# A hybrid two-block network on one core: the second block's projections written between the levels of its gated recurrence

## The reference

```
h = concatenate([meta, x])                       # 16 + 256 rows
q_pre, f_pre, i_pre, og_pre, lx, ly, ga, gb = split(rmsnorm(h) @ w_in)
# branch a: gated recurrence, 4 heads of 128
f = lb + (1 - lb) * sigmoid(f_pre);  k = (1 - lb) * sigmoid(-f_pre)
S_t = diag(f_t) S_{t-1} + k_t v_t^T;  o_t = S_t^T q_t      # v = i_pre
o_a = rms(o) * norm_g * sigmoid(og_pre)
# branch b: causal convolution (4 taps), then a linear recurrence
xc = conv(lx);  r = sigmoid(xc W_r + b_r);  i = sigmoid(xc W_i + b_i)
a = exp(-8 r softplus(-lam));  h_t = a_t h_{t-1} + sqrt(1 - a^2) i xc
o_b = h * gelu(ly)
merged = sigmoid(ga) * (o_a @ w_up_a) + sigmoid(gb) * (o_b @ w_up_b)
x = x + merged @ w_out
x = x + moe(rmsnorm(x))                          # 32 experts, 2 per token
```

## Time and profile before

| what | value |
|---|---|
| time, median of 3 runs | 1804.78 us (1804.09 to 1807.98) |
| time of the profiled execution | 1802.93 us |
| its span in the trace | 1801.1 us |
| busy: PE, PEld | 1708.2 us (95%), 1065.5 us (59%) |
| busy: DVE, ACT, POOL | 564.9, 183.2, 73.7 us |
| mean granted TensorE clock | 0.979 |
| read from memory | 372.70 MB |

### The profile page before, as it was taken

How to read it: one execution, slowest core, us unless ns; L and a number is a source line. 1 busy time by engine, 2 the same in 40 slices (tenths; PEclk the granted TensorE clock), 3 DMA queues, 4 the chain that set the end, 5 groups by cost and what they waited for, 6 DMA issues and landing times.

```text
span 1801.1 us, 16957 instructions
## 1 busy us (share of the span) xinstructions
PE 1708.2 (95%) x7316; PEld 1065.5 (59%) x7316; DVE 564.9 (31%) x1057; ACT 183.2 (10%) x284; POOL 73.7 (4%) x92
## 2 busy tenths in 40 slices
PE   7999999999999999999999986897879999999997
PEld 3865498864467647888446465786443444444442
DVE  3886120000259722000003127355332212122222
ACT  1311000000122110000011212141000000000000
POOL 2100020000010001000000012000000000000000
PEclk9999999999999999999999989898979999999999
DMA  5522465433444245444344331242749999999994
GB/s 172 196 94 97 148 174 166 141 140 119 163 141 140 94 140 175 141 142 174 128 163 140 111 123 47 71 142 92 321 190 429 427 428 428 428 426 428 427 428 189
DMA packets 116435, 374.86 MB, mean 208 GB/s; under 512 B 9780, under 2 KB 57400, under 8 KB 104328
## 3 DMA queue, kind: packets, MB, share of 16 engines
q1 hardware_dynamic: 112736, 370.36, 54.0%
q0 software_dynamic: 1248, 2.69, 0.8%
q10 hardware_dynamic: 2376, 0.72, 0.2%
HBM read 372.70 MB, written 1.05 MB: 208 GB/s over the span
## 4 chain that ended last, share of the span: by engine, by line
PE 90%; DVE 3%; ACT 2%; DMA 2%; issue 1%; POOL 1%; ACTq 0%; POOLq 0%; SPq 0%; DVEq 0%
PE bank L628 18%; PE bank L842 17%; PE bank L1068 11%; PE bank L576 11%; PE bank L587 7%; PE bank L1111 6%; PE bank L952 4%; PE bank L1047 3%; PE bank L1078 3%; PE bank L1011 2%; DMA arena<-in_w_up 2%; PE bank L595 1%; PE bank L967 1%; PE bank L897 1%; ACT arena L1147 1%
## 5 line engine op out<-in xcount | busy, mean ns | idle before, releaser
L842 PE MATMUL bank<-xT,weights 128*128 128x256 f32 (+1 forms) x1536 | 305.7, 362 | 1.9 <-DVE h L1396 1.9
L842 PEld LDWEIGHTS bank<-xT,weights 128*128 128x128 f32 x1536 | 271.8, 190 | 36.5 <-issue 3.5
L576 PE MATMUL bank<-weights,xT 128*128 128x512 f32 x448 | 197.0, 597 | 0.8 <-DVE xT L1388 0.8
L1068 PE MATMUL bank<-arena,mix 128*64 128x512 f32 x640 | 167.8, 592 | 1.8 <-DMA arena<-in_w_up 1.1
L628 PE MATMUL bank<-weights,arena 128*128 128x512 f32 x384 | 165.6, 592 | 0.0
L576 PEld LDWEIGHTS bank<-weights,xT 128*128 128x128 f32 x448 | 85.0, 192 | 103.3 <-issue 102.0
L628 PE MATMUL bank<-weights,xT 128*128 128x512 f32 x320 | 139.1, 593 | 2.6 <-ACT arena L1147 2.6
L587 PE MATMUL bank<-xT,weights 128*128 128x256 f32 (+1 forms) x576 | 128.0, 383 | 0.0
L628 PEld LDWEIGHTS bank<-weights,arena 128*128 128x128 f32 x384 | 72.6, 190 | 90.0 <-issue 89.9
L1068 PEld LDWEIGHTS bank<-arena,mix 128*64 128x64 f32 x640 | 54.6, 137 | 110.9 <-issue 110.0
L587 PEld LDWEIGHTS bank<-xT,weights 128*128 128x128 f32 x576 | 108.9, 190 | 18.2 <-issue 1.8
(11 more groups left out here) (391 smaller groups left out, 1455.0 us busy)
## 6 DMA issues: line engine op xcount, KB each, us to landing
weights<-in_w_in SPq DMA_DIRECT2D x30, 2048.0 KB, 8.0
arena<-in_w_gate SPq DMA_DIRECT2D x20, 2048.0 KB, 17.4
arena<-in_w_up SPq DMA_DIRECT2D x20, 2048.0 KB, 20.3
arena<-in_w_down SPq DMA_DIRECT2D x20, 2048.0 KB, 22.9
weights<-in_w_gate SPq DMA_DIRECT2D x12, 2048.0 KB, 18.1
weights<-in_w_up SPq DMA_DIRECT2D x12, 2048.0 KB, 20.3
weights<-in_w_ffn_gate SPq DMA_DIRECT2D x22, 1024.0 KB, 5.4
weights<-in_w_ffn_up SPq DMA_DIRECT2D x22, 1024.0 KB, 8.0
```

The costliest lines, as they stand in the source:

```text
L576: ins = mm(b[:, :], xT[:, k, t0 + P * t:t0 + P * t + P], w[:, k, :], start=(k == 0), stop=(k == KD - 1))
L842: ins = mm(b[:, 256 * q + n0:256 * q + n1], w[:, k, P * (f % 2):P * (f % 2) + P], xT[:, k, NM + n0:NM + n1], start=(k == 0), stop=(k == KD ...
L1068: ins = mm(psum[bank][SL * e:SL * e + SL, :], xsE[:, k, SL * e:SL * e + SL], w[e][:, k, :], start=(k == 0), stop=(k == KD - 1), skip_group ...
```

## The change

The list of tiles is new, and with it TensorE's order. `lx` is written in pairs of tiles, one pair ahead of each of levels 0 to 3; the tiles of `hi` stand ahead of levels 4, 5 and 6, `hog` ahead of the state products and behind level 7; unit 0 ahead of `ho`, units 1 and 2 behind it, 3 behind `oaT`, and 4 to 11 together behind `lr`. `ua` and `ub` come last. `wlev`, `qlev` and `klev` exist twice (the second set in `spare`, the last 4096 columns of the arena, which are also the experts' `early_slot`). The product for `klev` moves from GpSimd to VectorE; level i's result is added after level i + 1's operands. The gates' Sigmoids read the banks directly. The state tiles are added to `S` at the end of the levels. The convolution is split in six channels ahead of the norm of `ho` and two behind it. Gelu's first half stands ahead of the gates' chain, in a buffer of its own, and the softplus of lambda and the bound's Sigmoid move into the first block. The merged sum is handed over in four pieces, and `wo2` waits for each piece where it needs it.

```diff
 SECOND_TILES = (
-    [("m1", 4), ("hf", 4), ("hq", 2), ("hi", 3), ("hog", 2), ("lx", 8), ("hkm", 1), ("hk0", 1), ("hsm", 1), ("hs0", 1)]
-    + [tile for i in range(N_LEVELS) for tile in [(("lev", i), 2)] + unit_tiles(UNITS_AFTER[i])]
-    + [("ho", 2)] + unit_tiles(UNITS_NORM) + [("oaT", 2)] + unit_tiles(UNITS_CONV) + [("lr_r", 8), ("lr_i", 8), ("ua", 4)]
-    + unit_tiles(UNITS_LRU) + [("ub", 4), ("wo2", 4), ("m2", 4), ("rt", 1), ("rk", 1)]
+    [("m1", 4), ("hf", 4), ("hq", 2)]
+    + [tile for i in range(4) for tile in ((("lx", i), 2), (("lev", i), 2))]
+    + [(("hi", 0), 1), (("lev", 4), 2), (("hi", 1), 1), (("lev", 5), 2), ("hkm", 1), ("hk0", 1), (("hi", 2), 1), (("lev", 6), 2),
+       (("hog", 0), 1), ("hsm", 1), ("hs0", 1), (("lev", 7), 2), (("hog", 1), 1)]
+    + unit_tiles(0, 0) + [("ho", 2)] + unit_tiles(1, 2) + [("oaT", 2)] + unit_tiles(3, 3) + [("lr_r", 8), ("lr_i", 8)]
+    + unit_tiles(4, 11) + [("ua", 4), ("ub", 4), ("wo2", 4), ("m2", 4), ("rt", 1), ("rk", 1)]
 )
...
-        wlev = mflat[:, 0:1024].rearrange("p (a b) -> p a b", a=HG_H)
-        qlev = mflat[:, 1024:2048].rearrange("p (a b) -> p a b", a=HG_H)
-        klev = mflat[:, 2048:3072].rearrange("p (a b) -> p a b", a=HG_H)
+        spare = arena[:, 22400 - SLOT:22400]
+        wlev = [heads(mflat[:, 0:1024]), heads(spare[:, 0:1024])]
+        qlev = [heads(mflat[:, 1024:2048]), heads(spare[:, 1024:2048])]
+        klev = [heads(mflat[:, 2048:3072]), heads(spare[:, 2048:3072])]
...
+            sp.wait_ge(sem("lru_ready"), 1)
             expert_load(0, 0, 0)
             ring_free(0)
             expert_load(1, 1, 0)
-            sp.wait_ge(sem("merged_ready"), 1)
+            sp.wait_ge(sem("merged_ready"), 4)
...
-                g.tensor_tensor(klev, kT[:, :, NM:NTOK], wlev, ALU.mult).then_inc(sem("klev_ready"), 1)
...
+            for i in range(4):
+                lx_out(i)
+                level(i)
+            rows_of("hi", 0, ch + 4)
+            level(4)
...
+            ch = rows_out(TILE["wo2"], ch, KD, lambda k, t: mTt[:, k, P * t:P * t + P], 2, lambda: turn(TILE["m2"], xn, 0, "xn_ready"),
+                          ahead={0: merged, 2: merged, 4: merged, 6: merged})
...
+            def level_in(i):
+                v.wait_ge(sem("w_ready"), n.next("w_ready"))
+                TT(qlev[i % 2], qT, wlev[i % 2], ALU.mult).then_inc(sem("dve_step"), 1)
+                v.wait_ge(sem("dve_step"), n.next("dve_step"))
+                TT(klev[i % 2], kT[:, :, NM:NTOK], wlev[i % 2], ALU.mult).then_inc(sem("level_ready"), 1)
+                v.wait_ge(sem("level_ready"), n.next("level_ready"))
...
+            for i in range(1, len(LEVELS)):
+                level_in(i)
+                if i + 1 < len(LEVELS):
+                    level_diff(i + 1)
+                level_out(i - 1)
...
-            TT(mTt, ga, gb, ALU.add).then_inc(sem("merged_ready"), 1)
-            v.wait_ge(sem("merged_ready"), n.next("merged_ready"))
+                TT(mTt[:, 2 * i:2 * i + 2, :], ga[:, 2 * i:2 * i + 2, :], gb[:, 2 * i:2 * i + 2, :], ALU.add).then_inc(sem("merged_ready"), 1)
+                v.wait_ge(sem("merged_ready"), n.next("merged_ready"))
```

More of the change, by code:

```diff
@@ L957, in _, with rows_of, level @@
+            def rows_of(name, i, c_):
+                pe.wait_ge(chunk_full(c_), full_at[c_])
+                tile = TILE[name, i]
+                b = claim(tile)
+                n0, np_ = (NM + P * i, P) if i < NT else (0, NM)
+                for k in range(KD):
+                    ins = mm(b[0:np_, :], xT[:, k, n0:n0 + np_], slot(c_, KD, 512)[:, k, :], start=(k == 0), stop=(k == KD - 1))
+                ins.then_inc(psum_full(tile), 1)
+            def level(i):
                 if i < len(LEVELS):
-                    pe.wait_ge(sem("klev_ready"), n.next("klev_ready"))
@@ L959, in _ @@
-                    pe.wait_ge(sem("qlev_ready"), n.next("qlev_ready"))
-                    ka, qa = klev, qlev
+                    pe.wait_ge(sem("level_ready"), n.next("level_ready"))
+                    ka, qa = klev[i % 2], qlev[i % 2]
                 else:
@@ new lines, in _ @@
+            ins.then_inc(psum_full(TILE["hkm"]), 1)
+            b = claim(TILE["hk0"])
+            for hh in range(HG_H):
+                ins = nc.tensor.transpose(b[:, P * hh:P * hh + P], ket[:, hh, :], ident[:, :])
+            ins.then_inc(psum_full(TILE["hk0"]), 1)
+            rows_of("hi", 2, ch + 4)
+            level(6)
+            rows_of("hog", 0, ch + 5)
+            pe.wait_ge(psum_free(TILE["hkm"]), fills(TILE["hkm"]))
+            pe.wait_ge(psum_free(TILE["hk0"]), fills(TILE["hk0"]))
@@ new lines, in _, with unit_out @@
+            ins.then_inc(psum_full(TILE["hs0"]), 1)
+            level(7)
+            rows_of("hog", 1, ch + 5)
+            ch += 6
+            unit_chunk = [ch + u // 2 + (u >= 4) for u in range(UNITS)]
+            def unit_out(u):
+                uc = unit_chunk[u]
+                pe.wait_ge(chunk_full(uc), full_at[uc])
+                b = claim(TILE["unit", u])
+                for m in range(2):
+                    for k in range(KD):
+                        ins = mm(b[:, 256 * m:256 * m + 256], slot(uc, KD, 512)[:, k, P * (2 * (u % 2) + m):P * (2 * (u % 2) + m) + P],
+                                 xT[:, k, NM:NTOK], start=(k == 0), stop=(k == KD - 1))
+                ins.then_inc(psum_full(TILE["unit", u]), 1)
@@ L1277, in _ @@
-            copy(vt[0:NM, 2, :], TILE["hi"] + 2, psum[(TILE["hi"] + 2) % NPS][0:NM, :])
-            for t in range(NT):
-                copy(og[:, t, :], TILE["hog"] + t, psum[(TILE["hog"] + t) % NPS][:, :], ACT.Sigmoid)
+            copy_pair(qT[:, 0:2, :], TILE["hq"])
+            level_exp(0)
             act.wait_ge(sem("gend_ready"), n.next("gend_ready"))
             act.activation(fT[:, :, 0:NM], fT[:, :, 0:NM], ACT.Exp)
-            act.activation(klev[:, :, 0:P], klev[:, :, 0:P], ACT.Exp).then_inc(sem("gend_exp"), 1)
@@ L1304, in _ @@
+            copy(ke0, TILE["hk0"], psum[TILE["hk0"] % NPS][:, :].rearrange("p (h d) -> p h d", h=4))
+            copy(vt[0:NM, 2, :], TILE["hi", 2], psum[TILE["hi", 2] % NPS][0:NM, :])
+            for t in range(NT):
+                copy(og[:, t, :], TILE["hog", t], psum[TILE["hog", t] % NPS][:, :], ACT.Sigmoid)
+            for u in range(4):
                 copy_unit(u)
```

347 lines of the change are left out of this document (173 added, 174 removed).

## The result

| what | value |
|---|---|
| changed kernel, median of 4 runs | 1749.36 us (1748.84 to 1749.88) |
| kernel before, 4 runs beside them | 1806.19 us (1804.09 to 1807.98) |
| ratio | 0.9686, 95% interval 0.9669 to 0.9703 |
| its profiled execution, span | 1749.88 us, 1748.1 us |
| mean granted TensorE clock | 0.989 (0.979 before) |

The change takes 3.1% off.

A forecast was written before the change was run, and what follows sets the result against it. TensorE's waits (44.9 us) and half clock (13.5) between first block and experts were the removable loss. Less a new 3.35 us wait, 55.0 us came off 1802.93: 1747.9 profiled, 1750 median, range 1744 to 1763.

The forecast's parts named there:

- The sum: From `hq` to the first router product: 58.4 us of waits and half clock, less 3.35 us new wait, gains 55.0 us.
- First level: Before level 0: operands ready at 1000.2, TensorE arriving at 1004.5, so no wait and 4.3 us spare.
- Further levels: Levels after the first: VectorE needs 6.7 us per turn against slots of 9.2 and 8.7 us; no wait.
- rival 1: Level loop: VectorE products at 2.75 us set the pace, costing 7 to 20 us, 1757 to 1770; 12 in 100.
- cost 0: Levels after the first: VectorE and ScalarE work is covered by the projection in each slot, adding 0 us.
- States, norm, convolution: From `ho` to the gates: `ho` ends at 1089.0, `oa` ready 1099.1, `xc_ready` 1109.2; all covered by units.
- The tightest point: Convolution's `xc_ready` at 1109.2 against the end of unit 3 at 1110.7: 1.5 us spare.
- Recurrence: Between gates and `ub`: 69.6 us of cover for a 38.6 us chain removes the 11.47 us wait, 30 us spare.
- Merge: At `wo2`: the 3.16 us wait goes, a new 3.35 us wait comes before the transposes, clock cost 0.
- the other end: Behind the new wait in `wo2`: 2.6 us if the transposes and last records run at half clock.
- Transfers, softplus, experts: Weight loads, softplus and Sigmoid in the first block, expert stage: 0 each; about 1 us if the activations aren't covered.

The follow-up runs named there:

- a_apart4: The changed kernel with `apart` set back from 2 to 4 in `wo2`, the four merge pieces kept: 1745.67 us.
- c_single: The changed kernel with one set of level buffers and the old order of the level loop, both products still on VectorE: 1749.68 us.
- bc_both: The changed kernel with one set of level buffers, the old level loop and the `klev` product back on GpSimd, new TensorE order kept: 1750.09 us.
- d_units: The changed kernel with units 4 to 9 moved ahead of `lr`, leaving units 10, 11 and `ua` between gates and `ub`: 1749.87 us.

## Why the prediction was right, point by point

I forecast 1750 us with 1744 to 1763; it is 1749.36.

- **The sum.** The stretch was to fall by 55.0 us and fell by 53.64. The work at full clock was put at 259.9 us; 264.69 less the wait of 3.22 and less 1.7 of half clock is 259.8, and a_apart4, which has neither, takes 259.60. Nothing else was lost. The waits of the kernel before add to 44.7 us, not 44.9, and the 5.9 us put "before the state products" stood before `ho`; neither moves the sum.
- **First level.** Operands at 1000.2 and TensorE at 1004.5 were forecast. The products ended at 999.99 and the level began at 1003.85: a spare of 3.9 us.
- **Further levels.** VectorE's 1.22 us for two products on end was right (1.23 in the rows), and a turn took 1020.78 - 1014.13 = 6.65 us against my 6.7. The end at 2.75 us, rival 1, did not come: GpSimd is at 0.00 in the stretch. c_single and bc_both show that cost 0 was a safe term, since even the loop of before fits these slots. So the reasons given for it, second buffers and adds a level later, were not needed; the projection in each slot was enough. For rival 1 the prediction counted half of VectorE's products and adds as slow; in the trace it is 7 of 21 (two products of 2.75 and 3.40 us, five adds of 2.15 to 2.46).
- **States, norm, convolution.** End of `ho` 1088.30 (forecast 1089.0), `oa` 1098.4 (1099.1), `xc_ready` 1106.47 + 1.57 = 1108.0 against `lr` at 1109.90: 1.9 us spare where I had 1.5. The tightest point was named rightly and held.
- **Recurrence.** No wait, as forecast, but with more behind it than I counted. I kept the chain at 38.6 us and found 30 us spare; it is 25.9 and `ub` starts 42.5 us after it. By d_units the eight moved units alone were not what removed the 11.47 us: the shorter chain needs only two of them. What I credited to the cover has two causes, of which each suffices: d_units shows it for the shorter chain; that the longer chain of before would be covered by the eight units is worked out from rows, not run. And the cover before was not 13.8 us but the 27.1 from the last gate copy to the end of unit 11 (38.6 less the wait of 11.47).
- **Merge.** The wait before `wo2` went, and the new one of 3.35 us came as 3.22. The term that was mis-sized is the clock behind it: I took 0 and kept 2.6 as the other end. From the transposes to the router it was 1247.39 - 1243.05 = 4.34 us where it was 2.63, so 1.7.
- **Transfers, softplus, experts.** No wait names a DMA in the stretch; the loads of `in_w_in` still land in 7.8 us (issued between 960 and 1170 us). The first block has 773.73 us busy for 773.72. The experts have 430.03 busy of 432 us for 430.22. Three zeros, all held.
- **The rest.** The profiled execution was to take 1747.9 us and took 1749.88. The stretch was 1.4 us longer than forecast (the clock's 1.7, less small change); it began 0.5 us earlier; and from the router to the end it is 1748.1 - 1247.39 = 500.7 where it was 499.6, 1.1 us that I had not counted. Of this, 0.7 is the clock: behind a wait of 2.9 us in both, the 32 products of the experts' gather (L1089) took 6.45 us at a granted clock of 0.57, and 5.72 us at 0.65 before. Another 0.3 is the wait ahead of the second half's transposes, 3.57 us where it was 3.23. The forecast of the median added 1.85 us for the distance between a profiled run and the median, which the changed kernel doesn't have (1749.88 and 1749.36); that and the 2.0 us missing in the sum cancel. The median was met to 0.6 us partly by luck; the spans say 2 us.

## What to carry to other kernels

When TensorE waits for operands that come from a chain of other engines, look first for work of TensorE that can stand between the consumers: here it took out the 13.2 us of waits that stand between the levels without it, and double buffers and a product moved to another engine added nothing that the runs can tell, though they are worth 17.6 us where the order is not changed. To know what the parts of a change are worth, undo them together as well as one at a time: two sufficient causes both look like little or nothing alone. And what even both together don't bring back, as the waits before level 0 and `ho` here, went by something else. When a handover is cut into pieces at the head of a stage, check the tail too: lowering `apart` from 4 to 2 put back 3.7 of the 5.0 us that the pieces had won.
